# Sparse-attention mixer of a twelve-phase transformer kernel: masks on the diagonal blocks only, compressed values of two heads in one product, a pair's outputs in one PSUM bank

## The reference

```
logits = einsum("bghtd,bgnd->bghtn", qc, k_cmp) * scale      # 15 compressed keys
p_cmp = softmax(where(valid, logits)) * valid
o_cmp = einsum("bghtn,bgnd->bghtd", p_cmp, v_cmp)
...
p_sel = softmax(where(smask, qc @ ks * scale)); o_sel = p_sel @ vs   # selected blocks
p_win = softmax(where(wmask, qc @ kw * scale)); o_win = p_win @ vw   # window
out = gc[..., 0:1] * o_cmp + gc[..., 1:2] * o_sel + gc[..., 2:3] * o_win
return out @ w_o
```

## Time and profile before

| | |
|---|---|
| runs | 1604.34, 1603.9, 1604.19 us |
| median | 1604.19 us |
| the profiled execution: its time | 1604.25 us |
| its span in the trace | 1602.4 us |
| TensorE busy | 1592.0 us, 99% of the span |
| DVE busy | 1208.4 us, 75% |
| ACT busy | 879.5 us, 55% |
| the loop over the units in nsa | about 1342 to 1402 us |

### The profile page before, as it was taken

One profiled execution on the slowest core, in us unless ns is written; L12 is line 12 of the kernel. 1 busy time (PEld: TensorE's weight loads), 2 busy tenths in 40 slices (PEclk: granted clock), 3 DMA queues, 4 the chain that ended last, 5 costly groups with the idle time before them and its releaser, 6 DMA issues.

```text
span 1602.4 us, 22407 instructions
## 1 busy us (share of the span) xinstructions
PE 1592.0 (99%) x9096; PEld 1372.5 (86%) x9097; DVE 1208.4 (75%) x1285; ACT 879.5 (55%) x1068; POOL 88.6 (6%) x103
## 2 busy tenths in 40 slices
PE   9999999999999999999999999999999999999999
PEld 7998888889888887888888888888888887788887
DVE  6687688865569887798787687975664577867886
ACT  6355655645555565565554456554443455855563
POOL 0233000000000000000000000000100002000000
PEclk9999999999999999999999999999999999999999
DMA  8435887584487656797365787547545562077861
GB/s 291 156 126 189 280 214 221 166 239 156 149 300 228 201 152 201 252 292 201 132 223 167 271 233 262 159 167 225 185 161 201 198 201 86 8 238 243 263 194 53
DMA packets 234616, 315.78 MB, mean 197 GB/s; under 512 B 7965, under 2 KB 185585, under 8 KB 231955
## 3 DMA queue, kind: packets, MB, share of 16 engines
q1 hardware_dynamic: 226026, 284.33, 53.3%
q0 software_dynamic: 2880, 20.97, 6.4%
q10 hardware_dynamic: 5608, 9.06, 2.2%
HBM read 290.75 MB, written 1.57 MB: 182 GB/s over the span
## 4 chain that ended last, share of the span: by engine, by line
PE 91%; DVE 4%; DMA 3%; ACT 1%; issue 1%; SPq 1%; POOL 0%; DVEq 0%; POOLq 0%; ACTq 0%
PE ps L2527 28%; PE ps L2531 15%; PE ps L2733 12%; PE ps L2696 6%; PE ps L2566 3%; PE ps L2555 3%; PE ps L2557 3%; PE ps L2518 2%; PE ps L2515 2%; PE ps L2516 2%; PE ps L2623 2%; PE ps L2624 2%; PE ps L2625 2%; DVE wlo L1607 1%; PE ps L2614 1%; PE ps L2858 1%
## 5 line engine op out<-in xcount | busy, mean ns | idle before, releaser
L1607 DVE TENSOR_TENSOR wlo<-raw,whi 128x2048 fp32r<-128x2048 f32 (+1 forms) x234 | 510.7, 2189 | 168.6 <-ACT whi L838 167.4
L2527 PE MATMUL ps<-x_both,whi 128*128 128x512 f32 x2080 | 496.8, 390 | 0.2 <-DVE silu L1798 0.2
L838 ACT ACTIVATE whi<-raw 128x2048 fp32r<-128x2048 f32 x223 | 422.1, 1904 | 120.1 <-DMA raw<-in_ffn_w_gate_up 49.1
L2527 PEld LDWEIGHTS ps<-x_both,whi 128*128 128x128 f32 x2080 | 386.0, 188 | 78.7 <-issue 0.9
L2531 PEld LDWEIGHTS ps<-x_both,wlo 128*128 128x128 f32 x2080 | 267.5, 191 | 10.6
L2531 PE MATMUL ps<-x_both,wlo 128*128 128x256 f32 x2080 | 270.7, 283 | 0.0
L1617 DVE TENSOR_TENSOR wlo<-arena,whi 128x2048 fp32r<-128x2048 f32 x70 | 159.9, 2284 | 14.1 <-ACT whi L855 14.1
L855 ACT ACTIVATE whi<-arena 128x2048 fp32r<-128x2048 f32 x70 | 133.9, 1913 | 3.8 <-DMA arena<-arena 3.8
L971 ACT ACTIVATE silu<-ps 128x512 f32<-128x512 f32 x50 | 29.8, 597 | 128.5 <-PE ps L2531 128.5
L2555 PE MATMUL ps<-whi,x_both 128*128 128x512 f32 x232 | 88.5, 392 | 0.1
L2515 PE MATMUL ps<-x_both,whi 128*128 128x256 f32 x352 | 88.4, 289 | 0.0
(11 more groups left out here) (335 smaller groups left out, 2361.9 us busy)
## 6 DMA issues: line engine op xcount, KB each, us to landing
raw<-in_ffn_w_gate_up SPq DMA_DIRECT2D x80, 1024.0 KB, 6.4
raw<-in_ffn_w SPq DMA_DIRECT2D x46, 1024.0 KB, 6.3
arena<-in_ffn_w_down SPq DMA_DIRECT2D x24, 1024.0 KB, 8.1
arena<-arena POOLq DMA_DIRECT2D x20, 1024.0 KB, 9.5
raw<-in_ffn_w_down SPq DMA_DIRECT2D x20, 1024.0 KB, 5.0
arena<-in_ffn_w SPq DMA_DIRECT2D x16, 1024.0 KB, 7.5
raw<-in_hgrn_w_in SPq DMA_DIRECT2D x14, 1024.0 KB, 5.5
raw<-in_moba_w_in SPq DMA_DIRECT2D x12, 1024.0 KB, 5.1
```

Source lines behind the costliest of these rows:

```text
L838: act.activation(whi[s % WRING][:, 0:width], raw[chunks.slot(n)][:, 0:width], ACT.Copy).then_inc(split_hi, 1)
L1607: ins = dve.tensor_tensor(wlo[s % WRING][:, part], raw[chunks.slot(n)][:, part], whi[s % WRING][:, part].bitcast(F32), ALU.subtract)
L2527: pe.matmul(ps[:, bank + n, :], hi[:, k, n * P:(n + 1) * P], x_both[:, k], start=k == 0, stop=k == KT - 1, skip_group_check=True)
```

## The change

Five edits, all in nsa.

1. The mask product writes blocks 0 and 2 of each bank only (2 x 128 columns instead of 384). Block 1 gets its first write from the product of the scores.
2. `vc` becomes a block-diagonal matrix: per group 2 x 64 columns, where partition blocks 0 and 2 hold the values in the first 64 columns and blocks 1 and 3 in the last 64, with zeros elsewhere. It is cleared by a memset of 128 x 512 ahead of the one of `cp`, and filled by four copies of 32 partitions instead of one of 128.
3. The four products of 15 rows (two heads, two query tiles) become one of 64 rows, 128 output partitions and 256 columns.
4. The outputs of a pair lie in one bank, 6 or 7 in turn, instead of half in each. The order of the six products of L3191 is unchanged.
5. The first `values` of a pair waits for `y_low` of the pair before the last, not of the last.

```diff
-        vc = area(5816, NG, HD)
+        vc = area(12800, NG, 2, HD)
...
         def nsa_out(pair):
-            return (lambda x: x[:, pair, :].rearrange("p (t s) -> p t s", t=TT)), ps[:, 6:8, 0:P]
+            return (lambda x: x[:, pair, :]), ps[:, 6 + pair % 2, 0:S]
...
                         dve.wait_ge(cmp_done, 2)
-                        dve.tensor_copy(vc[:], ps[:, 5, 0:NG * HD].rearrange("p (g d) -> p g d", g=NG)).then_inc(kc_kept, 1)
+                        for n in range(4):
+                            of_head = slice(32 * n, 32 * n + 32)
+                            ins = dve.tensor_copy(vc[of_head, :, n % 2, :], ps[of_head, 5, 0:NG * HD].rearrange("p (g d) -> p g d", g=NG))
+                        ins.then_inc(kc_kept, 1)
...
                 dve.wait_ge(gelu_ready, 2)
+                dve.memset(vc, 0.0)
                 link(dve.memset(cp[:], 0.0))
...
                     for a in range(2):
-                        pe.matmul(ps[:, first_bank + a, 0:3 * P], ident_b[:], mask_b[:], start=True, stop=False,
-                                  skip_group_check=True)
+                        diagonal = [v.rearrange("p (b s) -> p b s", b=3)[:, 0:3:2, :] for v in (ps[:, first_bank + a, 0:3 * P], mask_b[:])]
+                        pe.matmul(diagonal[0], ident_b[:], diagonal[1], start=True, stop=False, skip_group_check=True)
...
-            def values(u, pv, pair, first):
+            def values(u, pv, pair, first, outputs=1):
                 pe.wait_ge(pt_ready, at.att + u + 1)
-                if pair and first:
-                    pe.wait_ge(ylo_ready, at.y + pair)
+                if pair >= outputs and first:
+                    pe.wait_ge(ylo_ready, at.y + pair - outputs + 1)
...
-                        values(i - 2, pv, (i - 2) // branches, (i - 2) % branches == 0)
+                        values(i - 2, pv, (i - 2) // branches, (i - 2) % branches == 0, outputs=2)
...
-                    heads = [(a, ps[a * HD:(a + 1) * HD, 6:8, 0:P]) for a in range(2)]
+                    out = ps[:, 6 + pair % 2, 0:S]
                     if branch == 0:
-                        for t in range(TT):
-                            for a, out in heads:
-                                rows_c = slice(32 * ((2 * pair + a) % 4), 32 * ((2 * pair + a) % 4) + N_CMP)
-                                pe.matmul(out[:, t, :], vc[rows_c, g, :], cpt[rows_c, g, t * P:(t + 1) * P], start=True, stop=False)
+                        two = slice(64 * (pair % 2), 64 * (pair % 2) + 64)
+                        pe.matmul(out, vc[two, g].rearrange("p a d -> p (a d)"), cpt[two, g, :], start=True, stop=False, skip_group_check=True)
                     v = vn[:, branch, :, g * HD:(g + 1) * HD]
                     last = branch == 1
                     for t, keys, part in ((0, 0, 0), (1, 0, 1), (1, 1, 2)):
-                        for a, out in heads:
-                            mm = pe.matmul(out[:, t, :], v[:, keys, :], pt[:, a, part * P:(part + 1) * P], start=False,
-                                           stop=last and part != 1)
+                        for a in range(2):
+                            mm = pe.matmul(out[a * HD:(a + 1) * HD, t * P:(t + 1) * P], v[:, keys, :], pt[:, a, part * P:(part + 1) * P],
+                                           start=False, stop=last and part != 1, skip_group_check=True)
```

## The result

| | before | after |
|---|---|---|
| median of 20 executions each | 1604.26 us | 1605.55 us |
| lowest to highest | 1603.47 to 1605.82 | 1604.89 to 1612.57 |
| the profiled execution: its time | 1604.25 us | 1605.46 us |
| its span in the trace | 1602.4 us | 1603.7 us |
| executions of 1609 us or more | 0 of 20 | 6 of 20 |

The ratio of the mean times, after over before, is 1.0015, with an interval of 1.0009 to 1.0022. The forecast of a change that can't be told from none has failed. The predicted 1604.3 is 1.25 us short of the median.

A forecast was written before the change was run, and what follows sets the result against it. TensorE was taken as the bound, within a ring with DVE and ACT passing part of its saving. Copies +1.00, ahead -0.18, six laps -0.60, behind -0.08 gave +0.14 us: 1604.39, or 1604.3 as median; range 1602.8 to 1605.6.

The forecast's parts named there:

- the case that all of the saving is lost: Rival: mask and compressed products cost their entry, not columns, so only the copies' +1.0 us remains, 1605.2; chance 0.13.
- The copies: DVE at the loop's start, ahead of the first turn: three more copies of 0.33 us, +1.00 (bounds +0.75 to +1.26).
- What the longer wait does to the clock: TensorE's wait for vc at the loop's start: counted at its length only, with no term for the clock.
- The masks: TensorE in the loop: 0.05 us less per mask product, 0.10 per unit, in 13 units.
- The rival of slow masks: Split output slows each mask product by 0.30 us, +8.8 with the copies, 1613; chance 0.04.
- The compressed product: TensorE, per pair: one product of 0.50 us replaces four taking 0.58, saving 0.08.
- both loads would be exposed: Rival: uncovered weight loads make the new compressed product take 0.84 us, +1.8 in all, 1606.0; chance 0.07.
- The ring: Closed 6.17 us loop over ACT, DVE and TensorE lets 0.10 of 0.28 us saved per pair through; six laps -0.60.
- The chain in the loop no longer TensorE alone: Sign expected in the profile after: short TensorE waits before odd turns or scores, released by DVE or ACT.
- One bank and the later wait: Outputs of a pair and their wait for y_low: the old wait did not bind, so relaxing it frees nothing.
- The memset: DVE clearing vc: about 0.46 us, hidden where DVE idles 0.83 for POOL's root, so it costs nothing.
- Ahead of the ring and behind it: Before the first lap, one mask pair -0.10 and one compressed product -0.08 us; behind the laps, one compressed product -0.08.

The follow-up runs named there:

- experiment 1: The kernel before with its one copy of vc made as four of 32 partitions, old layout: median 1606.83 us against 1604.38, ratio 1.0013.
- experiments 4: The changed kernel with y_low of a pair done one step later on DVE: median 1604.77 us against 1604.38 for the kernel before, ratio 1.0000.
- experiment 6: The changed kernel with the old 384-column mask products: median 1609.6 us against 1604.55 for the kernel before, ratio 1.0025.
- Experiments 3: The changed kernel with six products of zeros ahead of TensorE's wait for vc: median 1605.65 us against 1604.38 for the kernel before, ratio 1.0005.
- experiment 10: The changed kernel with old 384-column masks and six products of zeros ahead of the vc wait: 1604.88 us against 1604.75 for the kernel before, ratio 1.0000.
- experiment 2: The kernel before with only the mask products cut to the diagonal blocks: median 1603.89 us against 1604.38, ratio 0.9994.
- 7: The kernel before plus short masks, one bank per pair, later wait and y_low one step later; old copy and four products: 1603.13 us against 1604.55, ratio 0.9989.
- experiment 8: The changed kernel with y_low later and the vc wait moved behind the second compressed scores: 1602.03 us against 1604.55 for the kernel before, ratio 0.9983.
- 9: The kernel of experiment 8 with vc filled by two 128-partition instructions instead of four copies: 1602.37 us against 1604.75 for the kernel before, ratio 0.9984.
- the last lot: The unaltered change run again beside the kernel before: median 1606.5 us of 11 against 1604.75, ratio 1.0013.

## Where the prediction was right and where it failed

The prediction failed: it called the change one that can't be told from none, and the kernel is slower by an amount clear of its interval. The form of the sum stood: slower at the start, faster in the ring. The median, 1605.55, still lies in the range, but by 0.05 us and by luck: its upper bound was made for the case that all of the saving is lost, and that is not what happened. The centre was 1.25 us low, because two terms were too small, another had the wrong sign, and one consequence of the first was put at nothing.

- **The copies: the step that failed in size.** "The time of such an instruction is set by the 256 elements of a partition": that holds for its duration (0.41 to 0.43, against 0.42), but it was counted at 0.33, the distance from the copy of 128 partitions to the next operation. A copy of 32 partitions followed by another holds DVE for 0.43. On the path to the first turn that is +1.30 instead of +1.00 (experiment 1: +1.30), just above the upper bound of this term, +1.26, which had rightly been made of the full durations.
- **What the longer wait does to the clock: the step that was missing.** The prediction costed TensorE's wait at its length and put its effect on the clock at nothing, without a reason. With a standstill of 1.95 to 2.15 us, where it was 0.66, the mean granted clock is 0.995 to 0.997 in 25 of 64 executions, and in the two of these that were traced (experiments 4 and 6) it is a fall to 0.50 right behind the standstill. In the 20 executions of the change the six long ones have a mean of 1610.04 and the others of 1605.45, so they add 6 x 4.6 / 20 = 1.4 us to the mean, more than half of what the ratio 1.0015 stands for (2.4 us). No rival held it. Experiments 3 and 10 show the cause: fill the standstill and the long executions are gone, 8 of 10 without the filling and none of 11 with it.
- **The masks: right**, 0.11 each, 0.107 saved per unit against 0.10. The rival of slow masks is refuted. (Of what the prediction held against it, the "full rate" of the L2950 transposes doesn't come out of the earlier trace rows: six take 0.81, 0.135 each.) The Trainium skill's sentence ("PSUM — Partial Sum Buffer", Specifications) that a non-contiguous pattern slows matmuls significantly does not hold for two runs of 128 elements: 0.22 for two in the chain after, 0.109 each, in proportion to 0.163 for 384 columns.
- **The compressed product: close by luck.** 0.52 against the predicted 0.50, so 0.06 saved instead of 0.08 a pair. But the 0.46 of work and 0.04 for entering were not what it is made of: it is 0.42 of work (experiment 10) and about 0.10 of waiting for `keep_probs` of the even unit, a path that the prediction didn't name. The rule in the Trainium skill ("TensorE: Matmul & The Clock Gate", Part 3, The mechanism) by which both loads would be exposed would have given 0.84; the trace shows 0.52, and 0.42 in experiment 10.
- **The ring: right**, and the best part of the reading. 0.60 was predicted for six laps, 0.69 came. The masks alone come within 0.12 of the whole change over six laps (experiment 2), and with `y_low` out of the ring the laps are 5.95 with the masks alone, all of their saving (7), and 5.89 with the whole change (4, 8, 9). "The chain in the loop no longer TensorE alone" was right: in the fourth lap it runs through ACT and DVE for 5.4 us, step by step as the ring was read; in the others it names TensorE, with small "issue" pieces.
- **One bank and the later wait: right that they free nothing by themselves**, and short of the rest: they are what lets `y_low` be moved.
- **The memset: right**, hidden. Two memsets now stand there, 0.48 and 0.91, and DVE still waits for POOL's root ahead of L2365.
- **Ahead of the ring and behind it: wrong by 0.12 and 0.29.** -0.18 was written for turn 0 to turn 1 and -0.06 came: the compressed product behind the L3132 products, of another shape, takes 0.63 there and not 0.50 (that the shape is the reason is only argued). Behind turn 13, -0.08 was written and +0.21 came. There TensorE goes on into the output projection (L2627), and its first product starts at 1394.07, right behind the last exponentials of unit 14, which end at 1394.01: the ring sets that place too. With `y_low` one step later (experiments 4, 8 and 9) the same stretch is 8.83, so all but 0.02 of the +0.21 goes with that step of the ring.

The sum with the measured terms: +1.30 - 0.06 - 0.69 + 0.21, which is +0.75 from three decimals, where +0.14 was predicted. Of the difference of 0.61, the copies are 0.30, the ring's laps -0.09, the two ends 0.41.

Three things stay open. The medians at a full clock rose by 1.2 us in the executions of the result and by 0.5 in the last lot, against 0.75 and 0.79 in the trace; in the traces of all kernels the first scalings of L2221 start anywhere from 1346.96 to 1349.17, behind work that is nearly the same in all, and nothing here separates that spread from the change. And what decides in which executions the clock falls is not known: 8 of 10 in experiment 6 and 11 of 31 in the change had the same standstill. And the standstill isn't needed for a fall: experiment 8's profiled execution had a short one without it, and 5 of 94 executions of the kernel before were at 0.997 or 0.998; whether these fell at the same place wasn't seen.

## What to carry to other kernels

An engine's saving counts up to the length of the ring that it works in: add up the steps from a buffer's use to its next use over all engines before counting it, and look for a step that can leave the ring (here `y_low`). A wait can also hide inside the duration of a product: compare the start of its first weight load with the end of what it needs. Where a change makes TensorE wait longer, look at the granted clock of many executions, not of one: here a standstill of 2 us cost 4 more in four of ten executions, and cheap products that nobody reads, or a wait moved behind work that is there anyway, take that away. And price many small instructions by the distance between two alike, not by the distance from one to something else.

## What the runs showed of the hardware that was not expected

- A DVE copy from PSUM of 32 partitions x 256 elements, followed by another, holds the engine for 0.43 us; the one of 128 partitions was followed by the next instruction after 0.33, and two multiplications of 128 x 256 took 0.79. Fewer partitions bought nothing.
- With a standstill of TensorE of 1.95 to 2.15 us, and TensorE busy before and after, the mean granted clock was below 0.999 in 25 of 64 executions; with 1.3 us or less, or with the standstill filled, in 1 of 77. In the two long executions that were traced the clock fell from 1.00 to 0.50 behind the standstill and came back some 10 us later, with TensorE at 100% in between.
- A product of 64 rows and 256 columns in two fp32 passes takes 0.42 us in the chain when its first weight load starts 0.09 behind the last score product (experiment 10), and 0.52 when the load has to wait until 0.20 behind it (the change); the chain shows no wait there.
- A bf16 product that writes two runs of 128 columns with a gap of 128 takes 0.109 us, as one of 256 in a row would by proportion.
